# Gathering and adding the rows of the first 14 experts in the second half of an expert loop

## The reference

```python
def hierarchical_moe(xn, w_rg, b_rg, w_re, b_re, w_g, w_u, w_d):
    ...                                    # g_sel: best group, top_i: best 2 of its 8 experts
    top_p = jax.nn.softmax(top_v, axis=-1) * g_w
    expert_idx = (g_sel[:, None] * EXPERTS_PER_GROUP + top_i).reshape(-1)
    ...                                    # token rows sorted by expert, in blocks
    def expert_block(args):
        xb, e = args
        hb = jax.nn.silu(xb @ w_g[e]) * (xb @ w_u[e])
        return hb @ w_d[e]
    ...
    y = y_pad[dest] * gates[order][:, None].astype(y_pad.dtype)
    out = jnp.zeros((t, d), xt.dtype).at[token_idx[order]].add(y)
...
x = x + hierarchical_moe(rms_norm_2(x, norm_ffn[l]), ...)
return rms_norm_2(x, norm_final)
```

## Time and profile before

| | |
|---|---|
| time, median of 3 runs | 2155.77 us (2153.36 to 2157.02) |
| the profiled execution: its own time | 2155.53 us |
| its span, first to last instruction | 2153.7 us |
| TensorE busy | 2057.9 us, 96% of the span |
| VectorE / ScalarE / GpSimd busy | 862.8 / 571.9 / 285.7 us |
| mean granted TensorE clock | 0.992 |
| expert loop, first group product to end of expert 31 | about 1549 to 2098 us |
| spare block, then tail | about 2098 to 2112 us, 2112 to 2153.7 us |

### The profile page before, as it was taken

One profiled execution on the slowest core, in us unless ns is written; L12 is line 12 of the kernel. 1 busy time (PEld: TensorE's weight loads), 2 busy tenths in 40 slices (PEclk: granted clock), 3 DMA queues, 4 the chain that ended last, 5 costly groups with the idle time before them and its releaser, 6 DMA issues.

```text
span 2153.7 us, 37635 instructions
## 1 busy us (share of the span) xinstructions
PE 2057.9 (96%) x15542; PEld 1145.1 (53%) x15542; DVE 862.8 (40%) x1464; ACT 571.9 (27%) x1044; POOL 285.7 (13%) x272
## 2 busy tenths in 40 slices
PE   6999999999999999998999999999799999999996
PEld 4445555656434445543446454565466666666652
DVE  2225530555566742886465641234611111111114
ACT  2123322423664220442134211143011111121113
POOL 0014410432330012005000000000100000000003
PEclk9999999999999999999999999999899999999999
DMA  8201221122205026200122102100699999999996
GB/s 308 91 23 44 103 79 39 64 83 80 69 0 156 30 89 147 74 1 0 39 79 98 50 1 78 42 30 40 233 385 410 407 407 413 411 407 412 404 374 241
DMA packets 108963, 346.78 MB, mean 161 GB/s; under 512 B 20216, under 2 KB 59536, under 8 KB 95952
## 3 DMA queue, kind: packets, MB, share of 16 engines
q1 hardware_dynamic: 64272, 274.98, 32.9%
q0 software_dynamic: 14528, 48.51, 6.7%
q10 hardware_dynamic: 30080, 22.18, 3.2%
HBM read 310.77 MB, written 40.24 MB: 163 GB/s over the span
## 4 chain that ended last, share of the span: by engine, by line
PE 76%; DMA 9%; DVE 8%; ACT 4%; issue 2%; POOL 1%; ACTq 0%; DVEq 0%; POOLq 0%; PEldq 0%
PE bank L646 27%; PE bank L1328 10%; PE bank L800 9%; DMA y_of_slot<-HT 8%; PE bank L652 6%; PE bank L1344 6%; ACT work L1432 3%; PE bank L826 2%; DVE work L1939 1%; PE bank L935 1%; PE bank L720 1%; PE bank L1140 1%; PE bank L940 1%; DVE O L1939 1%; PE bank L1334 1%
## 5 line engine op out<-in xcount | busy, mean ns | idle before, releaser
L646 PE MATMUL bank<-slots,HT 128*128 128x512 f32 (+2 forms) x960 | 350.8, 523 | 1.7 <-DVEq L144 1.1
L646 PEld LDWEIGHTS bank<-slots,HT 128*128 128x128 f32 x960 | 170.9, 191 | 164.5 <-issue 159.2
L1432 ACT ACTIVATE work<-bank 128x512 f32<-128x512 f32 (+6 forms) x223 | 116.6, 528 | 425.3 <-PE bank L646 193.8
L1432 ACT ACTIVATE HT<-bank 64x256 f32<-64x256 f32 (+2 forms) x215 | 92.1, 431 | 446.8 <-PE bank L1328 240.5
L1432 ACT ACTIVATE work<-work 128x1024 f32<-128x1024 f32 (+7 forms) x199 | 158.6, 808 | 170.8 <-DVEq L144 88.4
L1328 PE MATMUL bank<-slots,HT 128*32 128x256 f32 x3136 | 172.4, 379 | 2.1 <-DVE HT L2642 1.2
L646 PE MATMUL bank<-HT,slots 128*128 128x512 f32 (+2 forms) x432 | 167.4, 546 | 2.3 <-DVEq L1952 1.3
L1328 PE MATMUL bank<-work,HT 128*32 128x256 f32 x3072 | 169.2, 379 | 0.2 <-issue 0.2
L2717 POOL TENSOR_TENSOR work<-work 128x1024 f32<-128x1024 f32 (+4 forms) x80 | 120.2, 1502 | 356.1 <-DVEq L144 251.0
L2648 DVE TENSOR_TENSOR HT<-HT,bank 64x256 f32<-64x256 f32 x97 | 41.0, 423 | 277.2 <-ACT HT L1432 276.9
L1328 PEld LDWEIGHTS bank<-slots,HT 128*32 128x32 f32 x3136 | 102.1, 110 | 69.4 <-issue 1.4
(11 more groups left out here) (287 smaller groups left out, 2608.5 us busy)
## 6 DMA issues: line engine op xcount, KB each, us to landing
slots<-in_w_e_gate_dram SPq DMA_DIRECT2D x17, 2048.0 KB, 15.5
slots<-in_w_e_up_dram SPq DMA_DIRECT2D x17, 2048.0 KB, 20.2
slots<-in_w_e_down_dram SPq DMA_DIRECT2D x17, 2048.0 KB, 20.8
work<-in_w_e_gate_dram SPq DMA_DIRECT2D x16, 2048.0 KB, 15.7
work<-in_w_e_up_dram SPq DMA_DIRECT2D x16, 2048.0 KB, 20.3
work<-in_w_e_down_dram SPq DMA_DIRECT2D x16, 2048.0 KB, 20.8
slots<-in_w_in_dram SPq DMA_DIRECT2D x9, 2048.0 KB, 8.4
slots<-in_w_ada_dram SPq DMA_DIRECT2D x6, 2048.0 KB, 14.2
```

Of the source, the lines that this page charges most:

```text
L646: ins = pe.matmul(bank, lhsT, rhs, start=(n == 0), stop=(n == len(pairs) - 1))
L1432: return act.activation(o, i, f, bias=bias, scale=scale, **more)
```

## The change

It does five things.

1. Routing makes two lists out of one. `EARLIER` is 1 where a row lies in a block below 14. `slot_id` gets twice the size of `y_dram` added for those rows, so that the tail's gather leaves them out; `early_id` gets it for all others. `early_gates` and `late_gates` are the gates times `EARLIER` and times one minus it. VectorE has five small operations more.
2. In the last 8 turns of the loop (experts 16 to 31), now written out on VectorE and GpSimd, GpSimd starts two gathers per turn for one tile of 128 tokens, out of blocks 0 to 13 alone, behind the turn's first token gather. They wait once for the stores of experts 0 to 13, and from the third on for VectorE to have added the rows two turns back.
3. VectorE adds one such row per expert to `O` (one operation on 128x1024), a turn after its gather, behind its copy of the expert's result, and two at the end.
4. In the tail each gather has a semaphore of its own, and the products of the first row start before the second row has come. TensorE's four idle products are gone, and it waits for the 16 early additions ahead of the residual's products.
5. Tile 6 is added on VectorE too, so TensorE has four tiles (0, 2, 4, 7), whose residuals all fit into PSUM ahead.

```diff
-        BY_DVE = (1, 3, 5)
+        BY_DVE = (1, 3, 5, 6)
...
-            idle_products(banks[0], 4)
+            pe.wait_ge(early_added, 2 * NT)
             for n in range(4):
                 residual(n)
             pe.wait_ge(diags_ready, 1)
             for n, i in enumerate(SUMMED):
-                pe.wait_ge(combined[i], 32)
-                for half, bank in enumerate(sum_banks(n)):
-                    for x in range(2):
+                for x in range(2):
+                    pe.wait_ge(combined[i][x], 16)
+                    for half, bank in enumerate(sum_banks(n)):
                         ins = pe.matmul(bank, GATE_DIAGS[:, x * NT + i, :], YG[2 * i + x][:, half * HALF:(half + 1) * HALF],
...
-            copy(slot_id[:, :], SLOT)
+            ts(EARLIER, BLOCK_OF, float(EARLY), None, ALU.is_lt)
+            stt(slot_id[:, :], EARLIER, 2.0 * Y_ROWS, SLOT, ALU.mult, ALU.add)
+            ts(BEYOND, EARLIER, -2.0 * Y_ROWS, 2.0 * Y_ROWS, ALU.mult, ALU.add)
+            tt(early_id[:, :], SLOT, BEYOND, ALU.add)
+            tt(early_gates, gates2, EARLIER, ALU.mult)
+            tt(late_gates, gates2, early_gates, ALU.subtract)
...
+            def add_early(i, x):
+                dve.wait_ge(early_in[x][i % 2], 16 * (i // 2 + 1))
+                line(dve.scalar_tensor_tensor(out=O[:, i, :], in0=EARLY_ROWS[2 * (i % 2) + x],
+                                              scalar=early_gates[:, x * NT + i:x * NT + i + 1], in1=O[:, i, :],
+                                              op0=ALU.mult, op1=ALU.add), early_added)
+            for i in range(NT):
+                for x in range(2):
+                    expert(EXPERTS // 2 - EARLY_LOOPS + i, x)
+                    if i:
+                        add_early(i - 1, x)
+            for x in range(2):
+                add_early(NT - 1, x)
...
+            def gather_rows(rows, at, to, arrived, below=Y_ROWS):
+                pool.indirect_dma_start(to, None, y_dram[0:below], bass.IndirectOffsetOnAxis(ap=rows[:, at:at + 1], axis=0),
+                                        bounds_check=below - 1, oob_is_err=False).then_inc(arrived, 16)
...
+            for i in range(NT):
+                for x in range(2):
+                    e = EXPERTS - 2 * EARLY_LOOPS + 2 * i + x
+                    pool.wait_ge(tokens_turned, e + 1)
+                    pool.tensor_copy(index[x][:, :], token_list[:, e + 2:e + 3]).then_inc(index_ready, 1)
+                    pool.wait_ge(index_ready, e + 1)
+                    gather_block(x, XG[x], rows_gathered[x])
+                    if x == 0:
+                        for stored in y_stored:
+                            pool.wait_ge(stored, 64 * (EARLY // 2 + 1))
+                        if i >= 2:
+                            pool.wait_ge(early_added, 2 * (i - 1))
+                        for half in range(2):
+                            gather_rows(early_id, half * NT + i, EARLY_ROWS[2 * (i % 2) + half], early_in[half][i % 2], EARLY * CAP)
```

More of the change, by code:

```diff
@@ L564, in program @@
         R1, R2, R3, RG = temp(NT), temp(NT), temp(NT), temp(NT)
-        INDEX, RANK_OF, KE_OF, BLOCK_OF, ROW_OF, SLOT, BEYOND = (temp(2 * NT) for _ in range(7))
+        INDEX, RANK_OF, KE_OF, BLOCK_OF, ROW_OF, SLOT, BEYOND, EARLIER = (temp(2 * NT) for _ in range(8))
         assert at_tail[0] <= 15 * T - TAIL
@@ L587, in program @@
         rows_marked = sem("rows_marked")
-        combined = [sem(f"combine_rows{i}") for i in range(NT)]
+        combined = [[sem(f"combine_rows{i}{x}") for x in range(2)] for i in range(NT)]
         out_sem = [sem(f"out_stored{i}") for i in range(4)]
@@ L594, in program @@
         eps_col, other_half = col(1), col(NT)
+        EARLY = 14
+        EARLY_LOOPS = EXPERTS // 4
+        early_gates, late_gates = col(2 * NT), col(2 * NT)
+        early_id = ctx.enter_context(nc.sbuf_tensor("early_id", [P, 2 * NT], U32))
+        EARLY_ROWS = [work[:, TAIL + x * D:TAIL + (x + 1) * D] for x in range(4)]
+        Y_ROWS = EXPERTS * CAP + SPARE * TG
+        early_in = [[sem(f"early_rows_in{x}{n}") for n in range(2)] for x in range(2)]
+        early_added = sem("early_rows_added")
         GATE_DIAGS = cut(work[:, 16 * D:16 * D + 2 * NT * P], 2 * NT)
-        BY_DVE = (1, 3, 5)
+        BY_DVE = (1, 3, 5, 6)
         SUMMED = [i for i in range(NT) if i not in BY_DVE]
@@ L2653, in _, with expert @@
             block_ready(tokens_ready)
-            with dve.Fori(0, EXPERTS // 2) as it:
-                for x in range(2):
[L2656 to L2663, removed]
+            def expert(it, x):
+                for g in range(TGS):
+                    dve.wait_ge(silu_ready, it * 6 + 3 * x + g + 1)
+                    hidden_of(g, hidden_ready)
+                dve.wait_ge(tokens_turned, it * 2 + x + 2)
+                block_ready(tokens_ready)
+                dve.wait_ge(y_stored[x], it * 64 + 64)
+                dve.wait_ge(down_full, it * 4 + 2 * x + 2)
+                dve.tensor_copy(YO[x][:, HALF:HALF + QW], DOWN_BANKS[1][:, 0:QW]).then_inc(y1_out, 1)
+            with dve.Fori(0, EXPERTS // 2 - EARLY_LOOPS) as it:
+                for x in range(2):
+                    expert(it, x)
+            def add_early(i, x):
[10 more added lines that the diff above has]
+                add_early(NT - 1, x)
             spare = spare_count(dve)
@@ L2671, in _ @@
             for at in range(2 * NT):
-                ts(GATE_DIAGS[:, at, :], const("ident"), gates2[:, at:at + 1], None, ALU.mult)
+                ts(GATE_DIAGS[:, at, :], const("ident"), late_gates[:, at:at + 1], None, ALU.mult)
             line(dve.memset(ss[:, 0:2 * NT], 0.0))
@@ L2695, in _ @@
                 if i in BY_DVE:
-                    dve.wait_ge(combined[i], 32)
                     for x in range(2):
-                        stt(O[:, i, :], YG[2 * i + x], gates2[:, x * NT + i:x * NT + i + 1], O[:, i, :], ALU.mult, ALU.add)
+                        dve.wait_ge(combined[i][x], 16)
+                        stt(O[:, i, :], YG[2 * i + x], late_gates[:, x * NT + i:x * NT + i + 1], O[:, i, :], ALU.mult, ALU.add)
                     dve.sem_inc(tile_added, 1)
@@ L2871, in _ @@
             hear("dve")
-            with pool.Fori(0, EXPERTS // 2) as it:
+            with pool.Fori(0, EXPERTS // 2 - EARLY_LOOPS) as it:
                 for x in range(2):
@@ L2895, in _ @@
                 for x in range(2):
-                    pool.indirect_dma_start(YG[2 * i + x], None, y_dram,
-                                            bass.IndirectOffsetOnAxis(ap=slot_id[:, x * NT + i:x * NT + i + 1], axis=0))\
-                        .then_inc(combined[i], 16)
+                    gather_rows(slot_id, x * NT + i, YG[2 * i + x], combined[i][x])
         @block.sync
```

## The result

| | before | changed |
|---|---|---|
| median of 6 runs each, taken together | 2155.28 us | 2163.43 us (2158.05 to 2164.66) |
| ratio of the runs | | 1.0036, 95% interval 1.0024 to 1.0048 |
| profiled execution (its span) | 2155.53 (2153.7) us | 2160.82 (2159.0) us |
| first group product to VectorE's last copy in the loop | 548.3 us | 557.0 us |
| last copy to the tail's first gather | 14.5 us | 13.4 us |

The change is slower, by 7.8 us by the ratio. I had forecast 2153.6 us in a range from 2147 to 2161 us. In the two profiles the loop gives up 8.7 us, the tail takes back 4.0 and the stretch between 1.0. The loop's own start is 1.6 us later, most of it ahead of anything that the change touches.

The account below looks back on a forecast made before the run. The prediction took the loop to be bound by TensorE and the DMA engines together, the tail by DMA. Routing +0.2, loop +5.4 and tail -7.7 us made -2.1 us, so 2153.6 us, range 2147 to 2161 us.

Parts of the forecast that it names:

- less what is free near the end: Loop's end: 3.1 us of free DMA time in the last two experts and 3.4 us of spare-block weight room absorb delay.
- The price of 11.9 us for 4.02 MB: Loop: the early rows take 11.9 us of all 16 DMA engines, at 2.97 us per MB; 5.4 us remain as loss.
- the tail's term: Tail: fewer gathered bytes and earlier last products make it 7.7 us shorter, bounds -9 to -4.5 us.
- Rival A: Loop: stores wait their queue turn, copies delay TensorE before expert 23; +11.5 us there, 2159.8 us in all; chance 0.22.
- Landing: Tail: the sixteenth gather lands at 25.2 us after the first gather's start instead of 31.9, -6.7 us.
- The semaphore per row: Tail's last products: four of eight matmul records finish before the second row lands, -1.5 us taken.
- the half clock: Tail's last products: after longer idleness TensorE may run them at 1.2 GHz, up to +1.9 us, 0.2 us taken.
- Routing: Ahead of the first token scaling: five more VectorE operations, 1.05 us less 0.84 us of idleness, +0.2 us.
- VectorE in the loop: Loop: one 1.30 us addition per expert costs nothing; 0.6 us of cover at the spare block, 0 taken.
- GpSimd's waits: Loop: waits for stores and additions, between a turn's token gathers, make no token gather late; cost nothing.
- Rival B: Loop: it takes the bytes for nothing, costing 1 us, so -6.5 us in all, 2149.3 us; chance 0.27.
- rival C: Gathers: a row left out costs as much as one moved, about +9 us, 2165 us; chance 0.04.

Follow-up runs that it names:

- e7: The changed kernel with the two early gathers of a turn started one expert later, behind its second token gather: 2161.34 us, ratio 1.0044 to before.
- e8: Kernel before with rows of blocks below 30 for tiles 4 to 7 gathered behind the last token gather, none in the loop: 2152.11 us, ratio 0.9996.
- e14: As e13, but the first gathers ahead held until the last down products are over: 2153.31 us, ratio 0.9994 to before.
- e16: The changed kernel, unaltered, profiled a second time: 2163.01 us, loop 561.5 us, tail 37.8 us.
- e5: Weights loaded in 8 KB pieces, not 16: in the changed kernel 2166.35 us, ratio 1.0063; in the kernel before 2155.88 us, ratio 1.0013.
- e6: The changed kernel with four idle TensorE products ahead of the last tile's: 2161.95 us, ratio 1.0045 to before; tail 35.5 us.
- e4: The changed kernel without early gathers and additions, the first 14 experts' part left out of the result: 2152.98 us, ratio 0.9994 to before.
- e12: As e4, with tile 6 on TensorE and the idle products back: 2151.25 us, ratio 0.9993 to before.
- e2: The changed kernel with a threshold of 0: all its code runs, early gathers leave out every row, the tail gathers all: 2156.43 us, ratio 1.0011.
- e1: Kernel before with the tail's edits alone (semaphore per gather, tile 6 on VectorE, no idle products): 2153.93 us, ratio 0.9998.
- e9: As e8, but only tiles 6 and 7 gathered ahead, tile 6 on TensorE, idle products kept: 2155.68 us, ratio 1.0013 to before.
- e13: After e9: tiles 7 and 6 gathered ahead from the spare block's token turn on, tile 5 behind the spare block's gather: 2151.74 us, ratio 0.9988.

## Why the prediction was wrong

**The view of the bound was right.** Two full resources in the loop, a tail bound by DMA. The bytes came out as worked: q0 moved 4.37 MB in the changed tail.

**The step that failed: "less what is free near the end", 3.1 + 3.4 us.** The price of 11.9 us for 4.02 MB nearly stood: the loop lost 10.3 us over five profiles, 9.4 us counted from expert 16 on, where the sum had 5.4. But I took the delay for something that queues up and can be worked off in idle DMA time after 2061 us. It can't, because loads are asked for by TensorE's progress: gate and up weights of e + 2 when e's products are over. At expert 21 of the first profile the weights were 0.55 us late already; from there each delay of TensorE moved all later loads, and with them the idle window and the spare block's room, by the same amount. The trace shows both. The window is still at 0.92, at the same place of the loop too. And the spare block's up weights were asked for at 2092.01 us and not 2081.75, 10.3 us later, landed 12.9 us after that and not 13.0, and were needed at 2108.57 us: the room is 3.7 us, unused, where it was 3.5. What the loop could absorb was the room of each load and store by itself (3.7 us for up weights, the last microseconds to the store's edge), and that was used up in five experts in the first profile and in ten in e7. e8 and e14 show the other side: their loops lose nothing to gathers put at their end.

**That step alone does not explain the miss.** With 10.3 us in place of 5.4, the sum would have been +2.8 us, 2158.6 us, still inside the range. It takes a second one, the tail's term further below, to get to +7.

**Rival A** had the size (11.5 us in the loop, 2159.8 us) and the sign, and half of its mechanism. The path by which most of the delay reached TensorE is its path: copies that waited for stores beyond 10 us, 6.0 us of waits against 1.4 us for weights in the changed kernel, and all of the waits over 0.5 us in e16. But it came late, from about expert 26 and not 21. The sign that I had named, waits for copies by expert 22 with ScalarE's store waits past 10 us, did not come: the waits at experts 21 and 22 were for weights, and the store waits there 8.78 and 9.89 us. And the cause it gave, the stores' turn in the queue, is not needed for the loss: without any late store it was 13.9 us (e5). Its chance of 0.22 was too low, and its time too. Its slope was read too smoothly as well: the second line of the earlier trace rows is the longest wait and not the last (10.34 and 5.49 us follow), and in between the waits stay at 7.2 to 7.8 us for four experts.

**The second step that failed: the tail's term was twice too large**, -7.7 forecast, -4.0 and -3.9 us in the two pairs of profiles. Landing -5.5 and not -6.7 us: the starts stretched by 1.4 us. The semaphore per row, -1.5 us taken, brought nothing: the last tile's eight products ran without a gap between the rows. And the half clock, for which I took 0.2 us, cost 1.4 us (5.12 against 3.70 us; e6 wins it back in its profile). In time the tail may be worth less still (e4, e12: 0 to 3.5 us).

**Small terms.** Routing: from the operation ahead of `slot_id` to the first scaling of tokens it is 2.35 us and not 2.10, and VectorE's 0.84 us of idleness there is gone, as forecast (+0.2 us). VectorE in the loop: nothing, as forecast; at the spare block +0.44 us where 0 was taken. GpSimd's waits, up to 14 us long, held back no token gather for which TensorE then waited.

**Sum with what was measured:** 0.2 + 0.4 + 10.3 - 3.9 = +7.0 us, against 7.8 us by the ratio (5.2 to 10.4). Rival B falls (e2 against the changed kernel: the same code with the bytes costs the loop 10 us), rival C falls (e2: rows left out are free).

**Left open.** e2's median lies 2.5 us above e1's, and only 0.4 us of that was found in more than one profile. e4's profile says -3.9 us in the tail while its time says -0.3 (medians) or -1.3 us (ratio) in all. What ScalarE's table load at the start of each turn adds to the stalls was not tested. And the short stops of TensorE's weight loads in e9 and e13 (some also in e16) have no cause on record.

## What to carry to other kernels

Idle time of a resource behind the stretch where it is full can't be borrowed from inside that stretch, if its transfers are released by the engine that they delay: most of the added DMA time then comes out at the end (here 9 to 10 of 11.9 us). Ask of each "free" window who opens it, and whether that one is late too. Bytes that are moved belong where the DMA share is below 1 already (here between the last weights and the first gather, though no version here gained more than some 2 us by it), and engines that are thinned out for it may drop to half clock just when the last transfer lands. Which queue's lateness stops the engine says how the delay arrives and not what causes it: shift the lateness to the other queue and look whether the loss stays.

## What was not expected of the hardware

An indirect gather whose rows are all left out costs the full DMA engines nothing that can be seen: in e2, with 14 such gathers from 1822 to 2061 us, q0's 3584 packets and 3.44 MB took 4.7% of the time, against 4.3% for 1568 packets and 3.43 MB in before, and TensorE never waited. By that the 14 took some 1 us of DMA time in all, an estimate. Smaller packets changed which queue was late, not how much: 8 KB pieces took store waits from 10.5 us to none and cost before 2.5 us by the medians (0.6 to 5.0 by the ratio). And a short idleness has an echo: behind waits of 2.91, 3.23 and 4.59 us the next products ran 3.1, 1.3 and 1.4 us longer, at granted clocks of 0.78, 0.79 and 0.72, so part of them at 1.2 GHz.
